# Delta rule of a two-block transformer: four chunks with buffers of their own, started in two steps of one round counter

## The reference, cut to what matters

```
decay = exp(where(incl, gc[i] - gc[j], -inf))
a_low = where(strict, (k k^T) * decay * beta, 0)
uw    = triangular_solve(a_low + I, [v * beta, k * beta * exp(gc)])
qk    = (q k^T) * decay ; q_dec = q * exp(gc) ; k_dec = k * exp(gc[-1] - gc)
# the only step that goes from chunk to chunk, with the state S:
v_new = u - w @ S
o     = q_dec @ S + qk @ v_new
S     = S * exp(gc[-1]) + k_dec^T @ v_new
```

## Time and profile before

| | us |
|---|---|
| median of three runs | 1410.73 |
| the profiled execution, its own time | 1415.65 |
| its span in the profile | 1413.8 |
| PE busy in the span | 1183.2 |
| DVE, ACT, POOL busy | 822.3, 605.1, 137.2 |
| delta stage, first matmul of `gc` to the first of `w_out` | 938.8 to 1166.4 |
| all that comes after it | 1166.8 to 1413.8 |

### The profile page before, as it was taken

The page is one execution under the profiler, slowest core; times in us unless marked ns, Lnnn a source line. Parts: engine busy times, 40 slices in busy tenths (PEclk is TensorE's granted clock), DMA queues, the critical chain, the costliest instruction groups (busy, mean ns, idle before and its releaser), DMA issues.

```text
span 1413.8 us, 18768 instructions
## 1 busy us (share of the span) xinstructions
PE 1183.2 (84%) x7577; PEld 1037.0 (73%) x7577; DVE 822.3 (58%) x1281; ACT 605.1 (43%) x1052; POOL 137.2 (10%) x163
## 2 busy tenths in 40 slices
PE   2879888799999798569999969926599595699997
PEld 2849646699899698458999959925488494599996
DVE  7567554689896865447654476464444444444443
ACT  0422444554444455445455653342243222555443
POOL 0010254000000000000000001011620620000000
PEclk9998799899999899788999979955698697799999
DMA  9888301389997463225856514610000003156550
GB/s 353 282 277 277 147 1 60 121 281 348 349 358 263 140 199 102 87 75 194 292 188 227 182 39 143 207 47 2 0 1 1 0 1 98 66 182 197 188 179 30
DMA packets 138487, 218.56 MB, mean 155 GB/s; under 512 B 7057, under 2 KB 95505, under 8 KB 138017
## 3 DMA queue, kind: packets, MB, share of 16 engines
q1 hardware_dynamic: 138400, 217.36, 45.7%
HBM read 216.29 MB, written 1.05 MB: 154 GB/s over the span
## 4 chain that ended last, share of the span: by engine, by line
PE 66%; DVE 17%; ACT 7%; DMA 4%; issue 4%; POOL 2%; DVEq 0%; SPq 0%; ACTq 0%
PE bank L463 16%; PE bank L464 15%; PE bank L465 15%; DVE ada_acc L516 3%; DVE low L457 2%; PE bank L2071 2%; ACT high L451 2%; DMA ring<-mlp_w 2%; PE bank L2083 2%; PE bank L2079 2%; PE bank L488 1%; PE bank L2326 1%; POOL zb L1005 1%; DMA ring<-ada_w 1%; DMA ring<-ev_w_in 1%
## 5 line engine op out<-in xcount | busy, mean ns | idle before, releaser
L457 DVE TENSOR_TENSOR low<-ring,high 128x2048 fp32r<-128x2048 f32 (+1 forms) x139 | 317.7, 2287 | 293.0 <-ACT high L451 292.7
L451 ACT ACTIVATE high<-ring 128x2048 fp32r<-128x2048 f32 (+1 forms) x139 | 264.6, 1905 | 276.2 <-PE bank L465 188.4
L463 PE MATMUL bank<-act_high,high 128*128 128x256 f32 (+1 forms) x1112 | 326.2, 293 | 15.3 <-DVE act_low L1309 15.3
L464 PE MATMUL bank<-act_low,high 128*128 128x256 f32 (+1 forms) x1112 | 320.4, 288 | 0.0
L465 PE MATMUL bank<-act_high,low 128*128 128x256 f32 (+1 forms) x1112 | 320.4, 288 | 0.0
L463 PE MATMUL bank<-high,act_high 128*128 128x512 f32 (+1 forms) x632 | 235.8, 373 | 14.7 <-DVE ust L1656 10.9
L463 PEld LDWEIGHTS bank<-act_high,high 128*128 128x128 f32 x1112 | 218.8, 197 | 21.8 <-DVE act_low L1309 17.1
L464 PE MATMUL bank<-low,act_high 128*128 128x512 f32 (+1 forms) x632 | 233.3, 369 | 0.0
L465 PE MATMUL bank<-high,act_low 128*128 128x512 f32 (+1 forms) x632 | 233.1, 369 | 0.0
L464 PEld LDWEIGHTS bank<-act_low,high 128*128 128x128 f32 x1112 | 218.6, 197 | 2.7 <-issue 1.7
L465 PEld LDWEIGHTS bank<-act_high,low 128*128 128x128 f32 x1112 | 218.2, 196 | 0.0
(11 more groups left out here) (399 smaller groups left out, 1542.6 us busy)
## 6 DMA issues: line engine op xcount, KB each, us to landing
ring<-mlp_w SPq DMA_DIRECT2D x64, 1024.0 KB, 6.1
ring<-ada_w SPq DMA_DIRECT2D x48, 1024.0 KB, 6.8
ring<-w_up SPq DMA_DIRECT2D x16, 1024.0 KB, 5.5
ring<-w_down SPq DMA_DIRECT2D x16, 1024.0 KB, 5.0
ring<-od_w_in SPq DMA_DIRECT2D x12, 1024.0 KB, 5.3
ring<-w_in SPq DMA_DIRECT2D x11, 1024.0 KB, 5.7
ring<-ev_w_in SPq DMA_DIRECT2D x8, 1024.0 KB, 7.4
ring<-ev_w_out SPq DMA_DIRECT2D x4, 1024.0 KB, 7.6
```

What stands on the lines that cost most here:

```text
L451: e.activation(weights(c)[0], in_ring(("w", c)), ACT.Copy).then_inc(*act.up("high", c))
L457: e.tensor_tensor(low, in_ring(("w", c)), high.bitcast(F32), ALU.subtract).then_inc(*vec.up("low", c))
L463: e.matmul(out_, ah, bh, start=start, stop=False)
L464: e.matmul(out_, ah, bl, start=False, stop=False)
```

## The change: own buffers per chunk, and all chunks on one round counter

Each of the six chunks gets a set of buffers. The first real pair keeps the old set; the second real pair ("last") gets its own, mostly in the four slots of the weight ring; the meta chunks get small ones. Only the state is one per direction. All chunks run on one counter `n`: both meta chunks and the first real pair start at n = 0, the second real pair at n = 6. `R` and `K` become two rounds. The waits of ACT and POOL for the state of the chunk before are gone; what waits for it is PE's `vn` (`vec.at("s", before[k])`), as before. POOL makes `bv` and `bek` after the second level step, `kdec` and `qdec` two rounds later (for the second pair two levels later). The axial attention is advanced three pieces a round from n = 2 on. There are 25 rounds with work.

Because the ring's slots now hold buffers, the four weight loads that used to sit in them wait: OUT2+2 and OUT2+3 for the last `xT` of the second pair, MLP2 and MLP2+1 for its `o`. The load of `post_mix` is moved behind OUT2+1's.

```diff
+        first_bufs = [{n: mem.take(f"d0_{n}", 4, P) for n in BUFS},
+                      {n: mem.take(f"d1_{n}", 4, P, at=d1_at[i]) for i, n in enumerate(BUFS)}]
+        last_at = [{**{n: ring_at[(RING_AT["w", OUT2 + 2] + d) % SLOTS] + i * 512 for i, n in enumerate(("a", "aT", "lT", "w"))},
+                    **{n: ring_at[(RING_AT["w", OUT2 + 4] + d) % SLOTS] + i * 512 for i, n in enumerate(("x", "xT", "bek", "qdec"))},
+                    "bv": after_cols + 8 * L2 + d * 512, "qk": aqk_at + 816 + d * 512} for d in range(2)]
+        buf = {(d, t): (meta_bufs if t == 2 else first_bufs if t == d else last_bufs)[d] for d in range(2) for t in range(3)}
+        state = [first_bufs[d]["s"] for d in range(2)]
...
             for h in range(4):
-                e.matmul(b[0:n, h * P:h * P + C], B["w"][0:C, h, 0:n], M1, start=True, stop=True)
+                m = e.matmul(b[0:n, h * P:h * P + C], B["w"][0:C, h, 0:n], M1, start=True, stop=True)
+            m.then_inc(*pe.up("R", k))
+            yield
             b = ps.take(e, ("K", k), vec, "a", k)
...
             e.wait_ge(*pe.at("gc", k))
-            if k in before:
-                e.wait_ge(*vec.at("s", before[k]))
...
+                if l == rows_level:
+                    if not first:
+                        e.wait_ge(*pe.at("s", (d, 2)))
+                    e.tensor_tensor(B["bv"][0:C], tokens(1), per_head(beta), ALU.mult).then_inc(*pool.up())
                     e.wait_ge(*vec.at("bg", k))
-                    e.tensor_tensor(B["bek"][0:C], tokens(0), per_head(st[0:C, 4, :]), ALU.mult).then_inc(*pool.up())
-                    e.tensor_tensor(B["kdec"][0:C], tokens(0), per_head(st[0:C, 1, :]), ALU.mult).then_inc(*pool.up("kdec", k))
...
+        CHUNKS = (((0, 2), 0), ((1, 2), 0), ((0, 0), 0), ((1, 1), 0), ((0, 1), 6), ((1, 0), 6))
+
         def beside_axial(chunks, axial):
 
-            n = 0
-            for order in ORDERS:
-                live = [chunks(d, order[d], order == (0, 1)) for d in range(2)]
-                while live:
-                    live = [c for c in live if next(c, "end") != "end"]
-                    for _ in range(1 if n < 12 else 2):
-                        next(axial, None)
-                    n += 1
+            live, waiting, n = [], list(CHUNKS), 0
+            while live or waiting:
+                for k, start in [c for c in waiting if c[1] == n]:
+                    live.append(chunks(*k, k[1] == 2 or k[0] == k[1]))
+                waiting = [c for c in waiting if c[1] > n]
+                live = [c for c in live if next(c, "end") != "end"]
+                for _ in range(0 if n < 2 else 3):
+                    next(axial, None)
+                n += 1
...
+        DELTA_ENDS = {("w", OUT2 + 2): lambda: pe.at("xT", (0, 1), LEVELS - 1), ("w", OUT2 + 3): lambda: pe.at("xT", (1, 0), LEVELS - 1),
+                      ("w", MLP2): lambda: pe.at("o", (0, 1)), ("w", MLP2 + 1): lambda: pe.at("o", (1, 0))}
...
+                if item in DELTA_ENDS:
+                    e.wait_ge(*DELTA_ENDS[item]())
```

More of the change, by code:

```diff
@@ L263, in program @@
         c_exp = mem.take("c_exp", KT)
-        ring = [mem.take(f"ring{i}", SLOT) for i in range(SLOTS)]
+        ring, RING_ENDS = [], []
+        for i in range(SLOTS):
+            ring.append(mem.take(f"ring{i}", SLOT))
+            RING_ENDS.append(mem.at)
         highs = [mem.take(f"high{i}", SLOT, dtype=F32R) for i in range(2)]
@@ L1717, in program @@
         o_acc = mem.take("o_acc", QT, 512)
-        dst_ = [mem.take(f"d{d}_st", 6, 4) for d in range(2)]
+        dst_ = {(d, t): mem.take(f"d{d}{t}_st", 6, 4) for d in range(2) for t in range(3)}
         assert mem.at <= phase_base + 4640 + 2 * SLOT
@@ L2026, in per_head, with joined @@
             return c.unsqueeze(2).broadcast_to([c.shape[0], 4, P])
[L2028 to L2032, removed]
+        before = {(0, 0): (0, 2), (0, 1): (0, 0), (1, 1): (1, 2), (1, 0): (1, 1)}
+        def joined(k, l):
+            return buf[k]["lT" if l % 2 else "a"]
         def delta_tensor(e, d, t, first):
             C, back, cols_, real, v_ = of_chunk(d, t)
-            B, k = buf[d], (d, t)
+            k = (d, t)
+            B, S = buf[k], state[d]
             n_levels = LEVELS if real else 4
@@ L2045, in delta_tensor @@
                 e.wait_ge(*act.at("kv_tok", 0, 1))
+                e.wait_ge(*low_made(OUT2 + 1))
             e.matmul(b[0:C, 0:4], M1, g, start=True, stop=True)
@@ L2070, in delta_tensor @@
                 for h, o in enumerate(four(b)):
-                    m = e.matmul(o, joined(d, l)[0:C, h, 0:C], B["x"][0:C, h, 0:C], start=True, stop=True)
+                    m = e.matmul(o, joined(k, l)[0:C, h, 0:C], B["x"][0:C, h, 0:C], start=True, stop=True)
                 m.then_inc(*pe.up("w", k, l))
@@ L2108, in delta_tensor @@
                 if real:
-                    m = e.matmul(o, B["x"][:, h, :], B["s"][:, h, :], start=False, stop=True)
+                    m = e.matmul(o, B["x"][:, h, :], S[:, h, :], start=False, stop=True)
             m.then_inc(*pe.up("vn", k))
@@ L2248, in delta_gpsimd @@
             tokens = lambda kv: kv_tok[0:C, t, kv, :].rearrange("p (h c) -> p h c", h=4)
+            rows_level = 1 if first else 3
             e.wait_ge(*pe.at("gc", k))
-            if k in before:
-                e.wait_ge(*vec.at("s", before[k]))
-            e.tensor_copy(B["w"][0:C], per_head(g)).then_inc(*pool.up("w", k))
+            n = P if real else C
+            e.tensor_copy(B["w"][0:C], g.unsqueeze(2).broadcast_to([C, 4, n])).then_inc(*pool.up("w", k))
+            yield
             yield
@@ L2717, in post_mix_load @@
         def post_mix_load(e):
-            e.wait_ge(*act.at("normed", "b2", 2))
+            for d in range(2):
+                e.wait_ge(*pe.at("s", (d, 2)))
             e.dma_start(post_mix, I["norm_mix_post_2"][0].partition_broadcast(P)).then_inc(*landed.up("post"))
```

60 lines of the change are left out of this document (39 added, 21 removed).

## The result

The changed kernel takes 1394.77 us (median of 4 runs, 1390.44 to 1406.16) against 1412.34 for the kernel before beside it (4 runs, 1407.44 to 1418.94): ratio 0.986, 95% interval 0.982 to 0.990. It is faster, by 1.4%, but that is 17.6 us where 43 were forecast, and 1394.8 lies outside the range.

The account below looks back on a forecast made before the run. PE bounds the levels; gaps and low clock cost the rest. Opening to 977.3, plus 130.3 work, 4.9 half clock and 11 waits, ends the stage at 1123.5, saving 42.9 us: 1368 us, 8-in-10 range 1350 to 1392.

Parts of the forecast that it names:

- Engines beside it: Delta stage: DVE's 107 us and POOL's 73 hidden behind PE in the middle; thin in rounds 7 and 8, possibly 4 us.
- 130.3 + 4.9 + 11: From first real level product to stage end: PE's work at full clock, six groups at half clock, waits that stay, in us.
- Opening, DVE against POOL: First rotation on DVE beside POOL's six mask products: 4.5 us charged, bounds nothing and 8.3.
- turns: In the opening, DVE and POOL alternate during the first rotation, so the middle value, 4.5 us, was taken.
- the upper bound of 8.3: Opening: 6 x 1.38 us if DVE waits out each of POOL's six mask products.
- the sign of a right opening: First 128x128 product of L2092 starts at 975 to 980.
- the rest of the opening: Stage start 938.8 until DVE reaches x, undisturbed: gates, R, `a` and two rotations in DVE's order, to 970.7.
- The ring: Weight loads losing their prefetch, after the stage: cost nothing; up to 7.2 us if the cover were gone.
- the 247 us: Everything behind the delta stage keeps its instructions; forecast wrong if it changes by over 5 us.
- rival 2: Delta stage rounds coupled by hand-overs on four in-order lists, PE paying in each; saving 18.8 us, 1392; chance 0.22.
- Its sign: For coupled rounds: PE busy under 80% in the window from the first 128x128 product of L2092 to stage end.
- the four rivals: Packed better, 1352 (0.17); rounds coupled, 1392 (0.22); clock stays down, 1446 (0.04); second pair held to old pace, 1400 (0.05).

Follow-up runs that it names:

- e5: Changed kernel with POOL's masked products, rows, kdec and qdec replaced by memsets, each done twice, so POOL writes as long but reads nothing; 1366.3 us.
- e2: Changed kernel with POOL's masked products, rows, kdec and qdec replaced by single memsets of the same tiles, so POOL reads nothing; 1366.5 us.
- e4: Changed kernel with DVE's two small gate instructions removed: PE sums the later gates, ACT takes both exponentials, POOL multiplies by beta; 1388.6 us.
- e7: Changed kernel with e4's gates, and POOL's rows bv, bek and kdec of all six chunks made by ACT; 1378.3 us.
- e13: Changed kernel with POOL waiting for its own last product before each of the delta stage's SBUF products; 1382.9 us.

## Why the prediction was wrong

- **The step that failed: "Engines beside it".** It let DVE's 107 and POOL's 73 us be "hidden behind PE in the middle" and charged nothing for POOL's reads there, because each busy time fits under 185 us. Together they don't fit: what POOL reads holds DVE. From the first real level product to the end the stage took 165.0 us where 146.2 were forecast (130.3 + 4.9 + 11), and this is 18.8 of the 21.2 us that it is too long. The first row is the changed kernel, the second e5, the same rounds without POOL's reads:

```profile
992.30:1157.30 165.00, 145.19 (x1127) 126.39 (x1127) 93.61 (x180) 54.98 (x151) 59.06 (x52) 0.88 0.05 17
971.70:1118.40 146.70, 142.36 (x1127) 123.48 (x1128) 70.10 (x180) 54.78 (x151) 47.35 (x98) 0.94 0.06 20
```

  PE is idle 19.8 us instead of 4.3, for the two waits of 7.83 and 11.06 us behind DVE's long instructions (7.7 us too long in L2445, which took 0.28 in e2, 2.4 in L2449, 7.3 in L2204). DVE is busy 23.5 us more.
- **"Opening, DVE against POOL" was mis-sized, and luck hid it.** It expected "turns" and took 4.5 us; the first rotation lost 9.12 - 0.69 = 8.4, the upper bound of 8.3. Yet the first real product came 40.9 us after the first gate sum, inside the 36 to 41 that the prediction named as the sign of a right opening: the rest of the opening was priced 1.6 us too high (34.0 against e5's 32.4), and the sign was wide. The rule that stood beside the step (the Trainium skill, SBUF — State Buffer, "Who interferes with whom": the loser is blocked for the whole instruction) agrees with the trace in that DVE is held; it speaks of one instruction of the other engine, and that DVE waited out six and more in a row is shown by the trace alone. By the bound at the opening the forecast would have been 1372, still 23 us off. "Turns" is what the earlier trace rows show, and what the second pair's x did in the changed kernel too; it was not what the three small instructions and the first rotation met.
- **The clock came out lower through this**: the groups behind a wait for DVE ran at half clock (L2092 at 1010.74: 3.75 us for two groups, 2.33 at the same place in e5). In the stretch above PE is busy 2.8 us more than in e5 for the same products.
- **The rest of the sum held as a sum.** e5 takes 146.7 us for the forecast's 146.2, but its parts offset each other: PE is busy 142.4 us where 135.2 were forecast and idle 4.3 where 11 were. The ring, the 247 us and the dense end were right.
- **The rivals.** The result lies near rival 2 (1392), but not by its mechanism: in e5 the same rounds in the same order cost PE only 4.3 us of waits. Its sign, PE busy under 80% from the first real product on, isn't there either: 88%. The cause was in none of the four rivals.

What stays open: what decides between turns and a long hold. POOL's products stood back to back at the second pair's x as well, and there DVE waited for one at a time; in two of the three trains that held it, it got in before their end.

## What to carry to other kernels

Before two engines' work is overlapped, check not only that their busy times fit, but whether DVE has products with two SBUF operands where POOL reads SBUF; DVE's small instructions on the critical path are the victims. One train can cost more than it takes over: six POOL products held DVE 8.4 us, and made by DVE itself they would take 6 x 0.68 = 4.1 (an estimate from the earlier trace rows). Three cures were measured: take two-operand instructions off DVE (e4, 6.5 us of the stage), give POOL's per-token scalings to ACT, which has time (e7, 7.4 more), and put a wait between POOL's products (e13, 10.6 us for eight lines). But DVE's list is in order, so a product moved there must not stand ahead of what PE waits for next.

## What the runs showed of the hardware

- A DVE product of 128x4 or 16x128 elements took 7.2 to 8.0 us beside a back-to-back train of POOL's SBUF products, 0.15 to 0.3 alone; with some 0.1 us between POOL's products (e13), none took over 1.8. Beside another back-to-back train DVE's 128x512 products took 1.75 us each, one POOL product at a time.
- Only DVE's two-operand reads from SBUF were seen held; reductions from PSUM and from SBUF and products with an operand in PSUM kept their times (0.44, 0.28 and 0.69). POOL's memsets, which only write, held nothing. The same section of the Trainium skill's SBUF — State Buffer says both; these rows agree.
- POOL lost too: its two products of 16x64 took 3.19 us in e4 (975.42 on) beside DVE's four x products, against 0.59 later for two of the same size.
